# Reordering high and low parts in the odd rounds of latent attention, GpSimd subtractions in halves, and a sum written beside the negated maxima

## The reference, cut to what matters

```
h = x @ w_in                                  # cq | ckv | k_rope | gate
q  = (rmsnorm(cq,  q_norm)  @ w_q_up)         # 16 heads x (64 + 32 rotated)
kv = (rmsnorm(ckv, kv_norm) @ w_kv_up)        # 16 heads x (64 key + 64 value)
s  = [q | rope(q_r)] . [k | rope(k_r)] * scale, causal
o  = softmax(s) @ v
y  = (o * silu(gate)) @ w_out
```

## Time and profile before

| | us |
|---|---|
| runs | 1699.55, 1696.96, 1698.3 |
| median | 1698.3 |
| profiled execution, its own time | 1696.41 |
| its span, first to last instruction | 1694.3 |
| PE busy | 1654.3 (98%) |
| DVE busy | 785.9 (46%) |
| ACT busy | 767.5 (45%) |
| POOL busy | 613.0 (36%) |

### The profile page before, as it was taken

How to read it: one execution, slowest core, us unless ns; L and a number is a source line. 1 busy time by engine, 2 the same in 40 slices (tenths; PEclk the granted TensorE clock), 3 DMA queues, 4 the chain that set the end, 5 groups by cost and what they waited for, 6 DMA issues and landing times.

```text
span 1694.3 us, 24289 instructions
## 1 busy us (share of the span) xinstructions
PE 1654.3 (98%) x9349; PEld 1343.5 (79%) x9349; DVE 785.9 (46%) x2038; ACT 767.5 (45%) x1565; POOL 613.0 (36%) x298
## 2 busy tenths in 40 slices
PE   8999999999999999999999998999999999999998
PEld 7777779777888787778777788777788888888877
DVE  3777636566344434435777635888141111001052
ACT  4566634566243535524566634336753222222252
POOL 4323223332242323224322224693144444444423
PEclk9999999999999999999999999999999999999999
DMA  6322144323442312144222145432153333332322
GB/s 170 69 45 73 50 154 137 77 67 64 147 145 75 88 51 78 59 162 112 61 50 75 51 149 148 122 88 75 38 174 100 99 92 95 100 100 88 124 63 87
DMA packets 216047, 161.17 MB, mean 95 GB/s; under 512 B 53756, under 2 KB 197148, under 8 KB 215933
## 3 DMA queue, kind: packets, MB, share of 16 engines
q1 hardware_dynamic: 205904, 130.21, 27.5%
q10 hardware_dynamic: 9804, 29.38, 5.4%
q0 software_dynamic: 224, 0.03, 0.1%
HBM read 148.32 MB, written 11.14 MB: 94 GB/s over the span
## 4 chain that ended last, share of the span: by engine, by line
PE 81%; DVE 9%; ACT 6%; issue 2%; POOL 1%; DMA 0%; ACTq 0%; SPq 0%; DVEq 0%; POOLq 0%
PE banks L481 22%; PE banks L483 22%; PE banks L482 22%; PE banks L739 5%; PE banks L700 4%; PE banks L754 4%; PE banks L905 1%; PE banks L723 1%; ACT G L1613 1%; ACT AB L1484 1%; ACT w_hi L1354 1%; DVE misc L2622 1%; DVE AB L2228 1%; POOL w_lo L2817 1%; DVE QKl L2052 1%
## 5 line engine op out<-in xcount | busy, mean ns | idle before, releaser
L2817 POOL TENSOR_TENSOR w_lo<-w_raw,w_hi 128x1024 fp32r<-128x1024 f32 (+2 forms) x253 | 572.3, 2271 | 1050.6 <-ACT w_hi L1354 1039.4
L481 PE MATMUL banks<-XTh,w_hi 128*128 128x512 f32 (+5 forms) x1216 | 450.7, 371 | 7.2 <-DVE XTl L2287 2.0
L483 PE MATMUL banks<-XTh,w_lo 128*128 128x512 f32 (+5 forms) x1216 | 444.7, 366 | 0.0
L482 PE MATMUL banks<-XTl,w_hi 128*128 128x512 f32 (+5 forms) x1216 | 444.7, 366 | 0.0
L1354 ACT ACTIVATE w_hi<-w_raw 128x1024 fp32r<-128x1024 f32 (+4 forms) x254 | 250.3, 995 | 160.3 <-PE banks L483 107.7
L481 PEld LDWEIGHTS banks<-XTh,w_hi 128*128 128x128 f32 (+2 forms) x1216 | 228.2, 188 | 53.2 <-issue 11.2
L483 PEld LDWEIGHTS banks<-XTh,w_lo 128*128 128x128 f32 (+2 forms) x1216 | 228.2, 188 | 38.1
L482 PEld LDWEIGHTS banks<-XTl,w_hi 128*128 128x128 f32 (+2 forms) x1216 | 228.4, 188 | 36.1 <-issue 0.2
L481 PE MATMUL banks<-w_hi,OTh 128*128 128x512 f32 (+1 forms) x448 | 173.1, 386 | 1.9 <-DVE QKl L2052 1.8
L483 PE MATMUL banks<-w_hi,OTl 128*128 128x512 f32 (+1 forms) x448 | 167.9, 375 | 0.0
L482 PE MATMUL banks<-w_lo,OTh 128*128 128x512 f32 (+1 forms) x448 | 167.8, 375 | 0.0
(11 more groups left out here) (212 smaller groups left out, 2340.8 us busy)
## 6 DMA issues: line engine op xcount, KB each, us to landing
w_raw<-in_w_gate_up_dram SPq DMA_DIRECT2D x44, 512.0 KB, 3.8
w_raw<-in_fox_w_in_dram SPq DMA_DIRECT2D x30, 512.0 KB, 4.1
w_raw<-in_mla_w_in_dram SPq DMA_DIRECT2D x26, 512.0 KB, 4.9
w_raw<-in_w_in_dram SPq DMA_DIRECT2D x24, 512.0 KB, 3.9
w_raw<-in_w_down_dram SPq DMA_DIRECT2D x22, 512.0 KB, 3.5
w_raw<-in_swa_w_in_dram SPq DMA_DIRECT2D x20, 512.0 KB, 4.2
w_raw<-in_mla_w_out_dram SPq DMA_DIRECT2D x16, 512.0 KB, 3.7
x_spill<-AB ACTq DMA_DIRECT2D x16, 512.0 KB, 2.6
```

The source lines that it names most:

```text
L481: nc.tensor.matmul(o, ah, bh, start=first, stop=False, skip_group_check=True)
L482: nc.tensor.matmul(o, ah, bl, start=False, stop=False, skip_group_check=True)
L483: return nc.tensor.matmul(o, al, bh, start=False, stop=last, skip_group_check=True)
L2817: pool.tensor_tensor(view(w_lo, u, RING), view(w_raw, u, RAW), view(w_hi, u, RING).bitcast(F32), ALU.subtract).then_inc(lo_done, 1)
```

## The change

Four edits.

1. ACT, rounds 1 and 3: the query's high part comes ahead of the first of the two splits, and the first key's high part ahead of the second. Round -1 keeps its order.
2. DVE, rounds 1 and 3: the second key's low part comes behind `rope_sum`, ahead of `norm(i+1, 0)`; it was behind that norm. ACT's place of the second key's high part is not changed.
3. The negated maxima of the pairs without sinks (56 instructions) also write a sum, which nobody reads.
4. GpSimd's subtraction is two instructions, over half of the unit each (of the columns for a unit of one row block, of the row blocks otherwise); the semaphore is raised by the second.

```diff
-        unused = sb("unused", [P, T])
+        unused = sb("unused", [P, 2 * T])
...
                     elif i % 2 and i < 5:
                         g = (i + 3) // 2
-                        if pos == 5:
+                        if pos == 5 and i < 0:
                             rope(g)
                             query(i + 3)
-                            if i > 0:
-                                keys(g, 0)
+                        elif pos == 5:
+                            rope(g)
+                            hi(QKh[:, 3 + (i + 3) % 2, :], group()[:, :])
+                            advance()
+                            hi(QKh[:, 2 * g % 3, :], group()[:, :])
+                            advance()
...
-                            ins = nc.vector.tensor_scalar(nb[:, b, ns], mx[:, b, ns], -pr.scale, None, ALU.mult)
+                            ins = nc.vector.tensor_scalar(nb[:, b, ns], mx[:, b, ns], -pr.scale, None, ALU.mult, ALU.add,
+                                                          accum_out=unused[:, 4 + 2 * b + x:5 + 2 * b + x])
...
                             if i > 0:
                                 keys(g, 0)
                             rope_sum()
+                            if i > 0:
+                                keys(g, 1)
...
                         elif pos == 2:
                             if i < 0:
                                 keys(g, 0)
-                            keys(g, 1)
+                                keys(g, 1)
                             rope_high(g)
...
-                pool.tensor_tensor(view(w_lo, u, RING), view(w_raw, u, RAW), view(w_hi, u, RING).bitcast(F32),
-                                   ALU.subtract).then_inc(lo_done, 1)
+                low, raw, high = view(w_lo, u, RING), view(w_raw, u, RAW), view(w_hi, u, RING)
+                nk, ncol = units[u][1], units[u][2]
+                for half in range(2):
+                    if nk == 1:
+                        at = (slice(None), slice(None), slice(half * ncol // 2, (half + 1) * ncol // 2))
+                    else:
+                        at = (slice(None), slice(half * (nk // 2), nk if half else nk // 2), slice(None))
+                    ins = pool.tensor_tensor(low[at], raw[at], high[at].bitcast(F32), ALU.subtract)
+                ins.then_inc(lo_done, 1)
```

## The result

The changed kernel takes 1705.3 us (median of 6 runs, 1702.6 to 1707.9) against 1698.05 for six runs of the kernel before on the same chip: a ratio of 1.0041, 95% interval 1.0025 to 1.0056. It is slower by 7.3 us; 1702.7 was predicted. This text quotes the profile of that execution. Of the runs of the next sections one was in the slow state (2328 us, of the kernel with halves alone) and has no part in its ratio.

A forecast was written before the change was run, and what follows sets the result against it. PE, busy 98% of the span, was taken as the bound, so only its waits count. +5.96 - 1.5 - 0.3 + 0.2 = +4.4 us gave 1700.8, with 1.9 to the median 1702.7; own range 1700.3 to 1705.5, 8 in 10 1696.2 to 1706.5.

The forecast's parts named there:

- `otmp` is as late as it may be: Second half of the values, odd latent rounds: PE starts 0.06 us behind `otmp`, so any delay of it moves PE equally.
- Edits 1 and 2, +5.96: Rounds 1 and 3 of both latent layers: second half of the values 1.23 and 1.75 us later, +5.96 us in all.
- The term for the changed `nb`, 0.15 a round: Negated maxima with a written sum, on DVE ahead of `otmp`: 0.07 us more each, 0.15 for two.
- Halves, -1.5 - 0.3 + 0.2: GpSimd halves: -1.5 us in two feed-forward norms, -0.3 among the index scores, +0.2 for remaining waits for low weights.
- The rival of the clock: PE's clock falls in each of four odd rounds while PE stands still: +11.2 us, 1709.5; chance 0.08.
- The first rival: Odd rounds: PE's small waits close (some 2.9 us), the second half of the values comes no later: 1693.9; chance 0.12.

The follow-up runs named there:

- halves alone: GpSimd's subtraction in two halves (edit 4) as the only change to the kernel before: 1697.7 us, ratio 0.9993 (0.9984 to 1.0002).
- both orders: The new orders of ACT and DVE (edits 1 and 2) together, against the kernel before: 1706.1 us, ratio 1.0044 (1.0031 to 1.0056).
- DVE's order alone: Second key's low part ahead of the norm on DVE (edit 2), the only change to the kernel before: 1701.9 us, ratio 1.0020.
- `otmp` delayed: Kernel before with two added VectorE operations of 128x512 ahead of `otmp` in the odd latent rounds: 1705.4 us, ratio 1.0038.
- the high part made first: The changed kernel, but ACT makes the second key's high part ahead of the exponentials of head 1; against before: 1697.8 us, ratio 0.9991.

## Why the prediction was right, point by point

- **`otmp` is as late as it may be: right.** A delay of 1.45 cost 1.43 a round.
- **The number: right, with some luck.** A difference of 4.4 was forecast and 7.3 measured; 1705.3 is just below the upper end of the forecast's own range, 1705.5. Two falls of the clock (3.2) and a longer wait (0.65) are not in the sum, and the halves gave more than was booked for them.
- **Edits 1 and 2, +5.96: right in mechanism, 0.3 too large.** Worked out: +1.23 and +1.75 a layer. Measured: +1.09 and +1.63, +1.19 and +1.70. The exponentials' start, 0.41 after the first high part's follower, and DVE's unbroken chain came out as written; the high part, expected at 130.08, started at 129.67, because PE had entered the round 0.4 earlier (a gain ahead of the layer, which I had not booked; all five kernels with halves gain 0.4 there, the others nothing). Counted from that entry, 0.14 is missing in round 1, and this is the `nb` term of the next point.
- **The term for the changed `nb`, 0.15 a round: wrong.** It was taken between zero and the price of a wide division. The line of the negated maxima in after, beside the earlier trace rows:

```profile
L2213 DVE TENSOR_SCALAR_CACHE_REDUCE nb<-mx x56: 150/155/159, 79.9 to 1206.5; 128x4 f32<-128x4 f32 x56
L2213 DVE DVE_READ_ACCUMULATOR nb<-mx x56: 81/83/85, 80.0 to 1206.6; 128x1 f32 x56
```

  The second row overlaps the next instruction. From the first maximum to `otmp` pass 134.02 - 133.03 = 0.99, before 0.98. The long ones of up to 1944 ns are gone, and PE gained nothing by it. It is edit 3 that takes them away: with it alone the longest is 159 ns, with the halves alone 890. By the Trainium skill ("SBUF — State Buffer", section "Who interferes with whom") the form that also writes its accumulator does not take the ports that VectorE shares with GpSimd; the trace agrees.
- **Halves, -1.5 - 0.3 + 0.2: right in the norms, incomplete.** The norms gave -0.73 and -0.60 where 0.75 each was booked, the second convolution -0.47. DVE in the last norm of the feed-forward, then POOL beside it, answering to the earlier trace rows:

```profile
1638.78 1.39 DVE L2306 SCALAR_TENSOR_TENSOR AB<-AB,inv 128x1024 f32<-128x1024 f32 x1
```

```profile
1635.29 8.55 POOL L2831 TENSOR_TENSOR w_lo<-w_raw,w_hi 128x512 fp32r<-128x512 f32 x6 [18.52 <-ACT w_hi L1354]
```

  The norm's instruction went from 2.35 to 1.39, and the price shows beside it: of the six halves the one that started at 1639.04 took 2.30, 1.0 more than the usual 1.29. 18 of the 446 halves of 128x512 took more than 1.35. Not seen: -0.34 ahead of each latent layer, and `rope_sum` in the odd rounds, which stood in the trace of before and was 0.4 to 0.8 longer there than beside halves. The change buried that gain under its own wait; alone it is worth 0.44 a round.
- **The rival of the clock, 0.08 for a fall in each round: not so, but the mechanism was at work.** Behind the waits of 1.8 to 2.0 us in the odd rounds of after and of the kernel with both orders the clock fell in 2 of 8, at 1.6 each. Behind those of 1.0 to 1.4 (DVE's order alone, `otmp` delayed) it fell in none of 8. I should have booked it as a part of the forecast (about one fall of 1.6), not as all or nothing. The row from which I took its price of 1.7 shows a fall that costs nothing (above): the size came out, but not from there.
- **The pooling: missed.** The traces of all five kernels with halves have a fall between 1118 and 1126 behind a wait of 1.9 us (L1161); none of the other seven, before among them, has it, where the wait is 1.7. The kernels with halves lose 1.8 there. That they bring it rests on this count; why the clock falls in the one case and not in the other is open.
- **The first rival, small waits that close for a gain: its condition was right.** It was to decide at a high part that ends by 129.43. With the high part made first (it ends at 128.86) nothing comes later than before. The rival's gain from closed waits is not shown: of the 1.1 us that the rounds gained, the halves alone account for all (1.8).

The sum by measured terms: +5.6 rounds, -2.2 halves (latents, convolution, norms, less 0.3 elsewhere), +3.2 for two falls of the clock, +0.65 at L1133: 7.3 us. That is 7.3 of the trace's 7.45; the second fall is counted with 1.6 and not with the pooling's 1.78. The predicted +4.4 lacks the falls and, with 0.65, the longer wait at L1133. The cause of this is open: over the same place the ten other kernels moved by -0.3 to +0.5 against before, some with halves and some without, so it cannot be put down to one edit.

## What to carry to other kernels

Before a wait is moved forward in an engine's order, look at when the thing waited for is made, and at what is queued behind: here one low part moved ahead of a norm cost 3.6 us in four rounds, and 5.6 with the other engine's order changed too; the same move with the high part made first on the other engine cost 0.7 in the rounds, measured against the halves alone (their medians are the same). When a resource comes due just behind something else that is as late, moving it alone gains little (0.16 a round); the moves in company show (0.95 a round, 0.44 of which the halves give alone). Compare a kernel of several edits with the kernel of each edit alone, and not only with the one before: a gain of one edit can hide the loss of another. An edit's worth depends on its company: the halves' 0.44 a round vanished behind the new wait.

## What the runs showed of the hardware

- A DVE addition of 128x512 with both inputs in SBUF (`rope_sum`) took 1.05 to 1.47 us in the odd rounds beside GpSimd's units of 128x1024, and 0.68 to 0.98 beside halves of 128x512. A scalar_tensor_tensor of 128x1024 took 2.35 before and 1.39 after, and 1.28 with no GpSimd instruction beside it.
- Splitting 253 GpSimd instructions in two added 43.7 us to its busy time, 0.17 us each; PE's waits for low weights fell from 2.2 to 1.0 all the same.
- An accumulated sum beside four columns costs nothing that can be seen: 155 ns at the median and an overlapped row of 83, against 166 for the plain form.
- The falls of PE's clock within these traces last 3.41 us, two of them 6.83. One of 3.41 cost 1.5 to 1.7 us where PE had work, and next to nothing ahead of a wait for another engine.
